# Moving two of fourteen VectorE tiles per step to one-column TensorE products in the modulation stage of a hybrid decoder layer

## What is computed

```python
mod = (jax.nn.silu(c) @ ada_w[layer] + ada_b[layer])[:, None, :]      # (2048) @ (2048, 12288)
sh1, sc1, g1, sh2, sc2, g2 = jnp.split(mod, N_MOD, axis=-1)           # six vectors of 2048
h = rms_norm(x, norm1_gain[layer]) * (1 + sc1) + sh1                  # x is (512, 2048), f32
proj = h @ w_in[layer]
```

## Time and profile before

| | us |
|---|---|
| median of 3 runs | 2345.07 |
| lowest and highest of them | 2342.13, 2352.10 |
| the profiled execution | 2342.15 |
| its span in the trace | 2340.3 |
| TensorE busy in the span | 2301.8 (98%) |
| VectorE busy in the span | 1634.8 (70%) |

### The profile page before, as it was taken

The page is one execution under the profiler, slowest core; times in us unless marked ns, Lnnn a source line. Parts: engine busy times, 40 slices in busy tenths (PEclk is TensorE's granted clock), DMA queues, the critical chain, the costliest instruction groups (busy, mean ns, idle before and its releaser), DMA issues.

```text
span 2340.3 us, 29124 instructions
## 1 busy us (share of the span) xinstructions
PE 2301.8 (98%) x10527; PEld 1873.4 (80%) x10527; DVE 1634.8 (70%) x2059; ACT 832.4 (36%) x1147; POOL 82.3 (4%) x80
## 2 busy tenths in 40 slices
PE   6999999999999999999999999999999999999998
PEld 5877887888876788788888888888888888888887
DVE  5978886586767433666777777786868686868683
ACT  4143325234146322443333333342424242424242
POOL 0012101021001000000000000000000000000000
PEclk8999999999999999999999999999999999999999
DMA  9976880867540243234544445353535353545452
GB/s 347 330 259 226 282 297 32 272 240 256 183 141 19 75 148 101 82 108 145 164 138 156 161 154 168 125 187 127 167 127 188 126 185 119 174 140 170 144 161 82
DMA packets 233746, 392.37 MB, mean 168 GB/s; under 512 B 16441, under 2 KB 108063, under 8 KB 232520
## 3 DMA queue, kind: packets, MB, share of 16 engines
q1 hardware_dynamic: 233672, 391.39, 50.5%
HBM read 382.93 MB, written 11.03 MB: 168 GB/s over the span
## 4 chain that ended last, share of the span: by engine, by line
PE 90%; DVE 5%; DMA 2%; issue 1%; SPq 1%; ACT 1%; DVEq 0%; ACTq 0%
PE PS L1077 12%; PE PS L1079 12%; PE PS L1078 12%; PE PS L1133 7%; PE PS L1134 7%; PE PS L1132 7%; PE PS L681 6%; PE PS L682 6%; PE PS L683 6%; PE PS L848 2%; PE PS L824 2%; PE PS L688 2%; PE PS L690 2%; PE PS L689 2%; DVE acc_first L1631 1%
## 5 line engine op out<-in xcount | busy, mean ns | idle before, releaser
L1472 ACT ACTIVATE whi<-stage 128x1024 fp32r<-128x1024 f32 x368 | 390.0, 1062 | 723.3 <-PE PS L1079 341.7
L2037 DVE TENSOR_TENSOR wlo<-stage,whi 128x1024 fp32r<-128x1024 f32 x368 | 448.8, 1221 | 119.6 <-PE PS L1079 115.1
L1077 PE MATMUL PS<-whi,xc_hi 128*128 128x512 f32 x1216 | 478.8, 394 | 0.8 <-DVE wlo L2037 0.4
L1079 PE MATMUL PS<-whi,xc_lo 128*128 128x512 f32 x1216 | 474.7, 390 | 0.0
L1078 PE MATMUL PS<-wlo,xc_hi 128*128 128x512 f32 x1216 | 474.3, 390 | 0.0
L1580 DVE TENSOR_TENSOR wlo<-stage,whi 128x1024 fp32r<-128x1024 f32 x136 | 169.2, 1245 | 211.1 <-ACT whi L1250 210.7
L681 PE MATMUL PS<-hhi,whi 128*128 128x512 f32 x768 | 309.3, 403 | 5.9 <-DVE wlo L1580 3.0
L683 PE MATMUL PS<-hhi,wlo 128*128 128x512 f32 x768 | 300.7, 392 | 0.0
L682 PE MATMUL PS<-hlo,whi 128*128 128x512 f32 x768 | 300.6, 391 | 0.0
L1250 ACT ACTIVATE whi<-stage 128x1024 fp32r<-128x1024 f32 x136 | 144.2, 1062 | 431.4 <-PE PS L683 302.9
L2088 DVE SCALAR_TENSOR_TENSOR xT<-PS,mod,xT 128x512 f32<-128x512 f32 x176 | 132.0, 750 | 227.9 <-PE PS L1134 227.9
(11 more groups left out here) (297 smaller groups left out, 2485.1 us busy)
## 6 DMA issues: line engine op xcount, KB each, us to landing
stage<-in_ffn_w_up SPq DMA_DIRECT2D x168, 512.0 KB, 4.1
ada_ring<-in_ada_w SPq DMA_DIRECT2D x128, 512.0 KB, 4.9
stage<-in_ffn_w_gate SPq DMA_DIRECT2D x128, 512.0 KB, 3.8
stage<-in_ffn_w_down SPq DMA_DIRECT2D x88, 512.0 KB, 4.6
stage<-in_w_in SPq DMA_DIRECT2D x80, 512.0 KB, 6.2
ada_first<-in_ada_w SPq DMA_DIRECT2D x64, 512.0 KB, 7.0
stage<-in_w_out SPq DMA_DIRECT2D x32, 512.0 KB, 4.3
xnat<-in_x SPq DMA_DIRECT2D x4, 1024.0 KB, 7.9
```

Of the source, the lines that this page charges most:

```text
L1077: mm(PS[:, b, :], x_hi, w, start=start, stop=False)
L1079: return mm(PS[:, b, :], x_lo, w, start=False, stop=stop)
L1472: f(whi_of(p).rearrange("p k n -> p (k n)"), slot_of(p), ACT.Copy).then_inc(w_hi, 1)
L2037: v.tensor_tensor(wlo[:, p % NW, :, :].rearrange("p k n -> p (k n)"), slot_of(p), whi_of(p).rearrange("p k n -> p (k n)").bitcast(F32), AL ...
```

## The change

`FIRST_DVE` goes from 14 to 12, and with it everything that is derived from it.

```diff
 P_SB = {3: 0, 2: 512, 1: 896, 0: 1152}
 ACW = 256
-FIRST_DVE = 14
+FIRST_DVE = 12
 ADA_STEPS = 128
 CMP_AT = (2, 6)
```

## The result

| | before | after |
|---|---|---|
| median of 20 runs, us | 2343.05 | 2351.31 |
| lowest and highest, us | 2339.78, 2357.12 | 2348.63, 2363.05 |
| profiled execution, us | 2342.15 | 2349.48 |
| span of its trace, us | 2340.3 | 2347.4 |

The ratio after to before is 1.0035, with a 95% interval from 1.0022 to 1.0048: some 8 us slower, a difference that the interval tells from none, and within the 0.5% of the prediction's middle case. The spans differ by 7.1 us. The traces are compared by these.

The account below looks back on a forecast made before the run. TensorE was taken as the bound, VectorE's saving worth only TensorE's wait: 12.9 - 1.84 - 0.97 + 0.15 = +10.2 us on 2342.15 gives 2352.4, set at 2353.5 towards the median's base; range 2346 to 2361.

Parts of the forecast that it names:

- the prediction's middle case: Whole kernel: no change that a measurement can tell, within about 0.5% (11.7 us); chance 0.57.
- What bounds the step: Modulation stage: TensorE and VectorE almost balanced, TensorE the larger part; VectorE's saving gains at most TensorE's wait, 1.84 us.
- The products: TensorE, modulation stage: 16 more instructions a step at 0.115 us, 1.84 us a step, 12.9 us in seven steps.
- The wait for the sums: TensorE waits for VectorE's last tiles ahead of the sums, 1.84 us in the whole stage; the change removes it.
- The wait ahead of L701: TensorE's wait for partial_out ahead of the first direct products, 0.26 us recorded: neither won nor lost.
- SyncE and the loads: SyncE's queue of buffer loads: one load could be late for VectorE's tile 8, costed at nothing given VectorE's slack.
- The clock in the loop: Step from 98.01: without its wait of 0.51 us the clock likely stays up, 0.97 us less.
- Rival B: Direct and sums stretch: one-column products thin the stream, clock falls to 1.2 GHz, 1.6 us each fall; chance 0.34.
- The first loop: Stage's start at the lower clock: two new one-column instructions perhaps twice as dear (0.23 us), 0.15 us added.
- Behind the stage: After the modulation stage: nothing touched by the change, the rest shifted as a whole, the stage's end 10 us later.
- The base: Profiled execution of 2342.15 us gives 2352.4, the median's base 2355.3; a value between, nearer the first, was taken.

Follow-up runs that it names:

- TensorE's part alone: Against the kernel before: TensorE issues eight extra one-column products a step into unread columns, VectorE keeps its 14 tiles; ratio 1.0041.
- 15 tiles: Against the kernel before: FIRST_DVE = 15, one tile moved back to VectorE, 4 direct products a step left on TensorE; ratio 1.0053.
- both orders changed: Against the kernel before, with 14 tiles: VectorE's tile 2 ahead of modulation from step 2 on, and partial_out right behind h_low; ratio 1.0003.
- the reordered kernel: Against the kernel before: the second unit's scores put ahead of the 128 products of 62 columns of the compression stage; ratio 0.9990.

## Why the prediction was right

It named 2353.5 us and no measurable change by the 0.5% bound, with slower next to it; the median is 2351.31 us and the ratio 1.0035. By its own steps:

- *What bounds the step* held: TensorE's list, with VectorE's part worth only the wait. TensorE's part alone gives the full 17.10 us.
- *The products*: 0.115 us each predicted, 0.110 measured, 12.3 us in seven steps and not 12.9. The Trainium skill's 62 ns (TensorE: Matmul & The Clock Gate, "Back-to-back issue gap") would have made it 6.9 us, an estimate; three step lengths with 0, 8 and 16 more instructions give 0.110. The trace has one weight load to each of these instructions, so it is likely that the loads are not hidden here, but no run separates load and product.
- *The wait for the sums*, 1.84 us: gone, as said. VectorE's idle time grew from 0.76 to 3.40 us a step, within the "2 to 3 us" more.
- *The wait ahead of L701*, costed at "neither won nor lost": 60.23 still shows it (0.28 us in brackets in the trace), and moving `partial_out` took 0.50 us out of the step.
- *SyncE and the loads*, costed at nothing: one load released a VectorE tile late, by 1.9 us in the first loop, and TensorE did not wait for the sums there.
- *The clock in the loop*: the prediction took it to stay up, 0.97 us less; the stretch reads 1.00 where it read 0.98. Rival B's fear that the products thin the stream until the clock falls is refuted for them: 112 more did not bring it about once in this profile. It is TensorE's waits that go with it, the reverse of the change. The prediction put the fall down to the longest wait; the later profiles do not bear out that the length decides.
- *The first loop* was the term furthest off: +1.84 + 0.15 = 1.99 us predicted, 0.56 measured. The lower clock at the start of the stage lasted 10.2 us in this profile and 13.7 us in the one before (the 0.87 and 0.73 of the stretches above). With 13.7 us again, TensorE's part alone had +1.66. That is chance of the run and not an effect of the change, as far as these profiles tell; with +1.66 in it the spans would be 8.2 us apart (an estimate), and the medians are 8.26 apart. The prediction said that no row prices a one-column instruction at the lower clock. Two in the kernel before do:

```profile
43.73 0.42 PE L701 MATMUL PS<-silu_c,ada_first 128*128 128x1 f32 x2
...
45.44 0.42 PE L701 MATMUL PS<-silu_c,ada_first 128*128 128x1 f32 x2
```

They are 1.71 us apart with three products of 512 columns at 0.43 between them, which leaves 0.21 us for each instruction. The 0.23 that was assumed was close.

- *Behind the stage* the prediction shifted all rigidly; 0.72 us were given back, mostly a wait for `wlo` at the start of a later group (L688), 1.0 us before and 0.2 after.
- *The base*: the value was put above the profiled sum of 2352.4 for the median's sake; with 20 runs the median of before was 2343.05, under the 2345.07 of the three.

Against the 7.1 us of the spans the sum of +10.2 is 3.1 too much: 0.73 in the six steps, 1.43 in the first loop and 0.96 ahead of and behind the stage. The mechanism was right, and no two large errors had to cancel; that the profile's difference came out as low as 7.1 is in part the chance of the first loop.

## What to carry to other kernels

Where two engines meet once a step, find the wait at the meeting point on both sides, from start to start: the smaller list can be relieved of any amount of work, and the step gains no more than the other engine's wait. A one-column product is not cheap on TensorE here: in float32 it is two instructions of 0.11 us, and each of them costs half as much as a product of 512 columns. And before moving work to get rid of a wait, ask what the clock does: a version with less work can be slower for the idle time that it brings.

## What the runs showed of the hardware

- Steps with a fall to 1.2 GHz followed on waits of TensorE from 0.3 to 2.5 us; a fall cost 0.97 us of the step in the kernel before, 1.5 with 15 tiles and 1.6 with both orders changed. Eight useless wide products in that place took 5.9 us out of the six steps with 15 tiles; two of them in a wait of 0.70 us changed nothing. The Trainium skill (TensorE: Matmul & The Clock Gate, "Why this matters for your kernels") warns of long idle gaps between bursts; here the fall also follows short waits among narrow products.
- A stretch of narrow products can hold the lower clock. A wait of 0.6 us for a load inside the group of 62-column products was followed by 0.21 us an instruction in place of 0.114, for the whole rest of it. A wait of 0.40 us at the same place in the changed kernel's profile was not (112 instructions in 13.05 us). The profiles at the two speeds are of different kernels; that this is also the 10 us between two runs of one program rests on the reordered kernel, whose upper group is gone. It is more than the change under study.
- The steps of the kernel with both orders changed did not vary around a mean: the last five settled at 17.0 us, with one fall in each, though the one step at full clock took 15.41.
- One-column instructions at the lower clock took 0.21 us each, against 0.11 at full clock.
- GpSimd working beside VectorE on the same kind of tile made VectorE's instructions 32% longer (745 to 984 ns).
